# Gate product in two passes over stacked weights, and the first projection unit begun on token block 0

## The reference

```
p = x @ w_in                    # columns: pool u | q | k | v | o | i gate (4) | f gate (4)
mLSTM: log f = log_sigmoid(f + bias), cumulative sums and running maxima of i and log f per head,
       decay weights exp(...) from them, matrix memory C, normaliser n, stabiliser m
pool:  trailing-window means (2/4/8/16) minus token, per-group map, scale
mix = concat(pool, sigmoid(o) * h) @ w_out
x1  = LayerNorm(alpha*x + mix)
x2  = LayerNorm(alpha*x1 + relu(x1 @ w_ff1 + b1)^2 @ w_ff2 + b2)
```

## Time and profile before

| | us |
|---|---|
| median of 3 runs | 1200.44 |
| lowest and highest | 1200.1, 1204.38 |
| span of the profiled execution | 1202.4 |

### The profile page before, as it was taken

How to read it: one execution, slowest core, us unless ns; L and a number is a source line. 1 busy time by engine, 2 the same in 40 slices (tenths; PEclk the granted TensorE clock), 3 DMA queues, 4 the chain that set the end, 5 groups by cost and what they waited for, 6 DMA issues and landing times.

```text
span 1202.4 us, 18123 instructions
## 1 busy us (share of the span) xinstructions
PE 1168.3 (97%) x7520; PEld 1148.5 (96%) x7520; DVE 515.7 (43%) x912; ACT 370.3 (31%) x610; POOL 96.3 (8%) x110
## 2 busy tenths in 40 slices
PE   7999999999999998999999999999999999999993
PEld 6999999999888998999999999999999999999993
DVE  5612222235665785433433433433433433433457
ACT  5622433322433665212212212203203203203222
POOL 4000000010011321000000000000000000000046
PEclk9999999998999999999999999999999999999997
DMA  8321111131045540210211201201201201201012
GB/s 240 83 57 36 38 36 38 36 108 36 18 157 160 185 153 36 71 35 36 70 36 35 70 33 37 70 24 46 70 11 59 70 1 68 70 0 70 1 44 98
DMA packets 63277, 76.41 MB, mean 64 GB/s; under 512 B 3241, under 2 KB 50441, under 8 KB 63220
## 3 DMA queue, kind: packets, MB, share of 16 engines
q1 hardware_dynamic: 59676, 65.12, 17.1%
q0 software_dynamic: 3552, 10.59, 3.0%
HBM read 69.04 MB, written 6.88 MB: 63 GB/s over the span
## 4 chain that ended last, share of the span: by engine, by line
PE 86%; DVE 5%; ACT 4%; issue 2%; DMA 2%; SPq 0%; ACTq 0%; POOL 0%; DVEq 0%
PE bank L1127 84%; PE bank L1131 2%; ACT w_hi L582 1%; DMA x_nat_all<-in_x_sample 1%; ACT x_T L607 1%; DVE y_acc L1062 0%; DMA x_nat<-in_x_prompt 0%; ACT relu L639 0%; DVE ln_stats L976 0%; DVE x_lo L1010 0%; DVE ln_stats L989 0%; DVE res_nat L1000 0%; SPq L247 0%; DVE w_lo L1018 0%; DVE ln_stats L977 0%
## 5 line engine op out<-in xcount | busy, mean ns | idle before, releaser
L1127 PE MATMUL bank<-x_hi,w_hi 128*128 128x344 f32 (+1 forms) x1464 | 476.5, 326 | 4.7 <-DVE x_lo L1010 3.0
L1127 PE MATMUL bank<-x_hi,w_lo 128*128 128x344 f32 (+1 forms) x1464 | 469.1, 320 | 0.0
L1127 PE MATMUL bank<-x_lo,w_hi 128*128 128x344 f32 (+1 forms) x1464 | 468.7, 320 | 0.0
L1127 PEld LDWEIGHTS bank<-x_hi,w_hi 128*128 128x128 f32 (+1 forms) x1464 | 275.1, 188 | 12.3 <-issue 3.8
L1127 PEld LDWEIGHTS bank<-x_hi,w_lo 128*128 128x128 f32 (+1 forms) x1464 | 274.8, 188 | 1.1
L1127 PEld LDWEIGHTS bank<-x_lo,w_hi 128*128 128x128 f32 (+1 forms) x1464 | 274.7, 188 | 1.0
L1127 PE MATMUL bank<-h_hi,w_hi 128*128 128x344 f32 x768 | 246.2, 321 | 0.8
L1127 PE MATMUL bank<-h_hi,w_lo 128*128 128x344 f32 x768 | 246.2, 321 | 0.0
L1127 PE MATMUL bank<-h_lo,w_hi 128*128 128x344 f32 x768 | 246.0, 320 | 0.0
L1062 DVE TENSOR_TENSOR y_acc<-y_acc,bank 128x344 f32<-128x344 f32 x192 | 95.9, 511 | 193.0 <-PE bank L1127 193.0
L582 ACT ACTIVATE w_hi<-w_raw 128x2048 fp32r<-128x2048 f32 x31 | 59.2, 1910 | 286.4 <-PE bank L1127 286.4
(11 more groups left out here) (216 smaller groups left out, 722.3 us busy)
## 6 DMA issues: line engine op xcount, KB each, us to landing
w_raw<-in_w_ff SPq DMA_DIRECT2D x32, 1024.0 KB, 5.3
w_raw<-in_w_out SPq DMA_DIRECT2D x12, 1024.0 KB, 4.9
w_raw<-in_w_in SPq DMA_DIRECT2D x16, 512.0 KB, 5.3
x_nat_all<-in_x_prompt SPq DMA_DIRECT2D x6, 512.0 KB, 7.6
x_nat<-in_x_prompt POOLq DMA_DIRECT2D x6, 512.0 KB, 4.8
out_y_prompt<-out SPq DMA_DIRECT2D x6, 512.0 KB, 2.6
w_raw<-in_w_in SPq DMA_DIRECT2D x2, 1024.0 KB, 5.9
sample_C<-in_state_C POOLq DMA_DIRECT2D x4, 512.0 KB, 6.8
```

Of the source, the lines that this page charges most:

```text
L1127: return nc.tensor.matmul(out, lhsT, rhs, start=start, stop=stop, skip_group_check=True)
```

## The change

1. **Gate product.** The gate weights get 100 columns: high parts in rows 0 to 3 and 32 to 35, low parts in rows 64 to 67 and 96 to 99. For each slice there are two matmuls instead of three (stacked weights by x high, stacked weights by x low), 16 per block instead of 24. The result goes to bank 7. ACT copies the two low rows groups to `gate_lo`, and DVE adds them, the high rows and the bias (`gate_rows_sum`), where ACT alone wrote the rows before.
2. **Order.** Unit 1's weights are fetched ahead of tiles 3 to 8. PE's list becomes `x_block(0)`, `gates(0)`, product 0 of unit 1, `x_block(1)`, product 1, `x_block(2)`, `gates(1)`, product 2, `gates(2)`, constants, products 3 to 5. The products of unit 1 now go block by block (f = i % 2, b = i // 2). ACT's and DVE's lists follow.
3. Unit 2's `split_hi` waits for the third gate product (its slot holds the gate weights), and the row results are transposed behind unit 2's fifth product.

```diff
@@ sync @@
-            for t in range(3, len(TILES)):
-                token_dma(sp, XNAT[0:TILES[t][1], t, :], a["x_prompt"], a["x_sample"], t, True, x_in[t])
             for u in range(1, U_OUT):
                 kind, j = PROJ[u - 1]
+                if u == 2:
+                    for t in range(3, len(TILES)):
+                        token_dma(sp, XNAT[0:TILES[t][1], t, :], a["x_prompt"], a["x_sample"], t, True, x_in[t])
                 if u >= 2:
                     sp.wait_ge(lo_done, u - 1)
...
@@ scalar @@
+            def gate_lo_rows(b):
+                act.wait_ge(gate_done, b + 1)
+                if b:
+                    act.wait_ge(gate_sum, 2 * b)
+                A(GL[0:NH, 0, :], N_[64:64 + NH, 0:BLK], ACT.Copy)
+                A(GL[0:NH, 1, :], N_[96:96 + NH, 0:BLK], ACT.Copy).then_inc(gate_low, 1)
...
+            act.wait_ge(gate_sum, 2 * NBLK)
             A(TZ[0:NH, :], TF[0:NH, :], ACT.Abs).then_inc(act_row, 1)
...
@@ vector @@
+            def gate_rows_sum(b):
+                if b == 0:
+                    dve.wait_ge(bias_in, 16 * 3)
+                dve.wait_ge(gate_low, b + 1)
+                stt(TI[0:NH, blk(b)], N_[0:NH, 0:BLK], SMALL[0:NH, 0:1], GL[0:NH, 0, :], ALU.add, ALU.add).then_inc(gate_sum, 1)
+                stt(TF[0:NH, blk(b)], N_[32:32 + NH, 0:BLK], SMALL[0:NH, 1:2], GL[0:NH, 1, :], ALU.add, ALU.add)\
+                    .then_inc(gate_sum, 1)
...
@@ tensor @@
+                for k in range(KC):
+                    mm(N_[0:GATE_ROWS, 0:BLK], gslot(WH)[:, k, :], XH[:, k, blk(b)], k == 0, False)
+                    last = mm(N_[0:GATE_ROWS, 0:BLK], gslot(WH)[:, k, :], XL[:, k, blk(b)], False, k == KC - 1)
+                last.then_inc(gate_done, 1)
...
             x_block(0)
-            x_block(1)
             pe.wait_ge(lo_done, 1)
             gates(0)
+            pe.wait_ge(lo_done, 2)
+            first_unit(0)
+            x_block(1)
+            first_unit(1)
             x_block(2)
             gates(1)
+            first_unit(2)
             gates(2)
...
+            for i in range(3, 6):
+                first_unit(i)
...
-                    if u == 2 and i == 1:
+                    if u == 2 and i == 4:
```

More of the change, by code:

```diff
@@ L50 @@
 N_OUT = N_PROJ + NBLK * KC
-GATE_ROWS = 36
+GATE_ROWS = 100
 PAIRS = NCH // 2
@@ L133, in build_layer @@
         assert base + cur[0] <= nc.sbuf_usable_end, (base + cur[0], nc.sbuf_usable_end)
+        GL = at("gate_lo", [P, 2, BLK], o_lay)
         VM = at("v_masked", [P, 2, 4, P], o_lay)
@@ L162, in build_layer @@
         stT_ready, stT_read = sem("stT_ready"), sem("stT_read")
+        gate_done, gate_low, gate_sum = sem("gate_done"), sem("gate_low"), sem("gate_sum")
         act_row, dve_row = sem("act_row"), sem("dve_row")
@@ L368, in keep @@
                 for j in js:
-                    pool.wait_ge(gemm_read, N_GATE + 12 * h + 3 * j + 3)
+                    pool.wait_ge(gemm_read, N_GATE + (6 if h == 0 and j == 0 else 12 * h + 3 * j + 3))
                     G.tensor_copy(SM[:, j, h, :], QKV[h % 2][:, j, sa]).then_inc(smp_kept, 1)
@@ L441, in split_hi @@
                 act.wait_ge(raw_in[u % 2], RAW_AT[u])
-                if u >= 2:
+                if u == 2:
+                    act.wait_ge(gate_done, NBLK)
+                elif u > 2:
                     act.wait_ge(gemm_done, outputs_to(u - 2))
@@ L453, in _, with x_hi_part @@
             A(SMALL[:, 3:4], ONES[:, 0:1], ACT.Copy)
-            for s in range(2 * len(TILES)):
+            def x_hi_part(s):
                 t0, n = TILES[s // 2]
@@ L460, in _ @@
                   bank[3 + s % 4][:, :].rearrange("p (k n) -> p k n", k=4)[:, :, 0:n], ACT.Copy).then_inc(x_hi, 1)
[L461 to L474, removed]
+            def gate_lo_rows(b):
[4 more added lines that the diff above has]
+                A(GL[0:NH, 1, :], N_[96:96 + NH, 0:BLK], ACT.Copy).then_inc(gate_low, 1)
             def evac(u, i):
                 kind, j = PROJ[u - 1]
-                f, b = i // 3, i % 3
+                f, b = (i % 2, i // 2) if u == 1 else (i // 3, i % 3)
                 n = N_GATE + 6 * (u - 1) + i
@@ L491, in evac @@
                     A(Y[:, 4 + j, blk(b)], src, ACT.Sigmoid).then_inc(gemm_read, 1)
-            act.wait_ge(gemm_read, NBLK)
+            for s in range(6):
+                x_hi_part(s)
+            split_hi(0)
+            split_hi(1)
+            gate_lo_rows(0)
+            evac(1, 0)
+            for s in range(6, 12):
+                x_hi_part(s)
+            evac(1, 1)
+            for s in range(12, 18):
+                x_hi_part(s)
+            gate_lo_rows(1)
+            evac(1, 2)
+            gate_lo_rows(2)
+            act.wait_ge(stT_ready, 1)
+            A(CST[:, :], B_[:, 0:92], ACT.Copy).then_inc(stT_read, 1)
+            act.wait_ge(stT_ready, 2)
+            A(SPT[:, :, :, :].rearrange("p g b r -> p g (b r)"),
+              S_[:, :].rearrange("p (g n) -> p g n", g=4)[:, :, 0:NS * NBUF], ACT.Copy).then_inc(stT_read, 1)
+            act.wait_ge(gate_sum, 2 * NBLK)
             A(TZ[0:NH, :], TF[0:NH, :], ACT.Abs).then_inc(act_row, 1)
@@ L499, in _ @@
             A(TZ[0:NH, :], TM[0:NH, :], ACT.Ln, bias=1.0).then_inc(act_row, 1)
-            evac(1, 0)
-            evac(1, 1)
+            evac(1, 3)
             split_hi(2)
@@ L506, in _ @@
             A(RBH[0:NH, pr], TN[0:NH, pr], ACT.Copy).then_inc(act_row, 1)
-            evac(1, 2)
+            evac(1, 4)
             act.wait_ge(dve_row, ROW_Z)
@@ L547, in _ @@
                     act.wait_ge(consts, 4)
-                for i in range(3 if u == 1 else 0, 6):
+                for i in range(5 if u == 1 else 0, 6):
                     evac(u, i)
@@ L724, in after_rows @@
                 dve.wait_ge(dve_row, row_n[0])
-            V.memset(WL[:, 0, 0:KC * GATE_ROWS].bitcast(F32), 0.0)
             row(V.memset(WH[:, 0, 0:KC * GATE_ROWS].bitcast(F32), 0.0), ROW_PAD)
@@ L733, in _, with x_lo_part @@
             row(V.memset(RBL[:, :].bitcast(F32), 0.0), ROW_INV)
-            for s in range(2 * len(TILES)):
+            def x_lo_part(s):
                 t0, n = TILES[s // 2]
@@ L740, in _ @@
                                 XH[:, ks, t0:t0 + n].bitcast(F32), ALU.subtract).then_inc(x_lo, 1)
-                if s == 5:
-                    split_lo(0)
-            split_lo(1)
+            def gate_rows_sum(b):
[5 more added lines that the diff above has]
+                    .then_inc(gate_sum, 1)
+            for s in range(6):
+                x_lo_part(s)
+            split_lo(0)
+            split_lo(1)
+            gate_rows_sum(0)
+            for s in range(6, 18):
+                x_lo_part(s)
+            gate_rows_sum(1)
+            gate_rows_sum(2)
             dve.wait_ge(stT_read, 2)
@@ L1158, in gates, with unit_product, first_unit @@
                 pe.wait_ge(x_lo, 6 * b + 6)
-                split_product(bank[b][0:GATE_ROWS, 0:BLK], lambda k: gslot(WH)[:, k, :], lambda k: gslot(WL)[:, k, :],
-                              lambda k: XH[:, k, blk(b)], lambda k: XL[:, k, blk(b)], range(KC)).then_inc(gemm_done, 1)
+                if b:
+                    pe.wait_ge(gate_sum, 2 * b)
+                for k in range(KC):
+                    mm(N_[0:GATE_ROWS, 0:BLK], gslot(WH)[:, k, :], XH[:, k, blk(b)], k == 0, False)
+                    last = mm(N_[0:GATE_ROWS, 0:BLK], gslot(WH)[:, k, :], XL[:, k, blk(b)], False, k == KC - 1)
+                last.then_inc(gate_done, 1)
+            def unit_product(u, f, b, n, ks=range(KC), before=None):
+                pe.wait_ge(gemm_read, n - 2)
+                cs = slice(P * f, P * (f + 1))
+                return split_product(bank[n % 3][:, 0:BLK], lambda k: wslot(WH, u)[:, k, cs], lambda k: wslot(WL, u)[:, k, cs],
+                                     lambda k: XH[:, k, blk(b)], lambda k: XL[:, k, blk(b)], ks, before)
+            def first_unit(i):
+                n, f, b = N_GATE + i, i % 2, i // 2
+                unit_product(1, f, b, n).then_inc(gemm_done, 1)
+            pe.sem_inc(gemm_done, N_GATE)
+            pe.sem_inc(gemm_read, N_GATE)
             pe.wait_ge(consts, 1)
             x_block(0)
-            x_block(1)
             pe.wait_ge(lo_done, 1)
             gates(0)
+            pe.wait_ge(lo_done, 2)
+            first_unit(0)
+            x_block(1)
+            first_unit(1)
             x_block(2)
             gates(1)
+            first_unit(2)
             gates(2)
@@ L1245, in att3 @@
                 last.then_inc(num_ready, 1)
-            for u in range(1, U_OUT):
+            for u in range(2, U_OUT):
                 pe.wait_ge(lo_done, u + 1)
```

6 lines of the change are left out of this document (3 added, 3 removed).

## The result

| | before | after |
|---|---|---|
| median us | 1203.95 (6 runs, 1200.1 to 1204.92) | 1212.73 (6 runs, 1209.57 to 1214.94) |
| span of the profiled execution | 1202.4 | 1209.3 |

The ratio is 1.0079, with a 95% interval of 1.0057 to 1.010: slower, by 6.9 to 12 us. The forecast was 1212.1 in a range of 1207.0 to 1216.5. The kernel before measured 1203.95 over six runs, the first three among them, against the 1200.44 that the sum started from, so the difference came out smaller (9.5 us by the ratio, 8.8 by the medians) than the 11.7 forecast.

A forecast was written before the change was run, and what follows sets the result against it. PE, busy 97% of the 1202.4 us span, was taken as the bound. On the 1200.4 median, +7.7 for unit 2's later start and +4.0 for the slow clock gave 1212.1 us; range 1207.0 to 1216.5, held at 80%.

The forecast's parts named there:

- the two conditions for unit 2: PE can begin unit 2 only with unit 1 finished and unit 2's w_lo there, which before was 3.2 us early.
- Part 1: Gate in two passes: 100 columns cost no more; 8 matmuls fewer in each of 3 blocks remove 3.8 us of PE work.
- Part 2: First stretch: gate product from 10.9 to 13.4, ACT starts on unit 1's weights at 12.6, product 0 at 16.9 after 3.5 us pause.
- rival (b): SP's queue holds back unit 1's second weight transfer, delaying product 0 and all behind it: 1215.8 us; chance 0.07.
- Part 3: PE's list: last gate product ends at 39.5 against 29.2; unit 1 ends at 51.3, 1.0 us earlier than 52.3.
- Part 4: Row chain starts 10.3 us later, 0.5 added; unit 2's w_lo at 60.0, PE waits 8.7 us, +7.7 us.
- Part 5: Slow clock behind two pauses: 1.6 us for that ahead of product 0, 2.4 for the long w_lo wait, +4.0 together.
- (a): Rival: the stall comes without a slow clock, 1208.1 us; chance 0.12.
- (c): Rival: clock falls at every transpose block between products, twice more at 1.6 us: 1215.3; chance 0.03.
- (d): Rival: unit 2's w_lo is not held by the row chain; unit 2 begins at 51.3, time 1199.4; chance 0.04.

The follow-up runs named there:

- e9: e2 with 8 more matmuls ahead of each gate product, so each costs PE 24 as before the change: 1205.07 us, ratio 1.0011 to the kernel before.
- e5: Kernel before with the two-pass gate alone, the old order in all lists, second and third gate products in banks 0 and 1: 1202.36 us, ratio 0.9993.
- e2: e1 with the PSUM copies of unit 1's last two products and unit 2's first ahead of ACT's row work: 1202.21 us, ratio 0.9989.
- e7: e4 with the five transposes of constants directly behind the gate products, ahead of products 1 and 2 of unit 1: 1202.87 us, ratio 0.9992.
- e3: Changed kernel with the third gate product, in a bank of its own, ahead of product 2 of unit 1: 1211.55 us, ratio 1.0058.
- e4: e3 with product 1 of unit 1 behind the gate products too, only product 0 ahead of them: 1212.05 us, ratio 1.0076.
- e6: Changed kernel with 50 idle matmuls of 344 columns put into PE's wait for unit 2's w_lo: 1210.74 us, ratio 1.0074.
- e1: Changed kernel with unit 2's weight split (w_hi on ACT, w_lo on DVE) ahead of the row chain: 1205.14 us, ratio 1.0017.

## Why the prediction was right, point by point

**What bounds the kernel, and the two conditions for unit 2.** Right. All the difference up to unit 2's fifth product is when unit 2 begins and at what clock.

**Part 1, two passes.** Right: 100-column matmuls go at the same pace, 16 instead of 24. What they are worth depends on the pauses behind them: 2.6 us of 3.8 in e9, 0.5 in e5.

**Part 2, the first stretch.** Product 0 at 16.70 for 16.9. ACT took unit 1's weights at 12.41 in the changed kernel (I had 12.6), so rival (b), weights held up in SP's queue, did not come. SP's second issue for them lasted 4.2 us, against 8.5 before, and no semaphore wait is named for it; that a full queue holds it is likely, and no view says so. The biases landed at 19.2 as worked out, and delayed nothing there. One row of it was off: the gate product began at 11.66 and ran to 15.8, not from 10.9 to 13.4. Its matmuls start 0.29 us apart up to 14.64 and 0.157 from 14.86 on, which is the half clock and then the full one; the pause for `w_lo` hid all of that. The profile gives a granted clock of 1.00 for 9 to 14 all the same, as it does in the earlier trace rows for 4 to 9, where the first 24 transposes took 4.99 us and 8 more only 1.09. So at the very start the pace of the matmuls has to be read and not the granted clock, and the prediction's "1.00 in all stretches up to 52" says too much.

**Part 3, PE's list.** Constants at 39.13 for 39.5; `x_block` took 3.1 us each (20.58 to 23.71).

**Part 4, the row chain.** The addition by low rows and sums was guessed at 0.5 and was that: 44.95 + 1.07 - 39.13 = 6.9, against 6.4 before. From Ln to `w_lo`'s end 13.5, as before. Wait 8.43 for 8.7, shift 7.25 for 7.7. e2 and e7 show that it was this and nothing else. What the prediction had not seen is that the constants' copies on ACT are a second head of the chain; it did not matter there, since they come 0.5 us ahead of the last sum, but it decided e3 and e4.

**Part 5, the clock.** In the profiled execution its two terms were too large: 1.6 for the first pause was 0 (product 0 took 3.9 us, at full clock), and 2.4 for the long wait was 1.3 (e6 against the changed kernel). Neither is always so small: in e4, product 0 lasts from 16.66 to the transposes at 23.26, 6.6 us instead of 3.9, and the clock in it was the half one, and the long waits of e3 and e4 cost 2.6. The changed kernel's six runs lie in two groups, 1209.6 to 1211.1 and 1214.4 to 1214.9, with mean granted clocks of 0.989 to 0.990 and 0.984 to 0.985. What makes the two is open: only one of the six has a trace, and the six runs of the kernel before, which has no pause ahead of product 0, split as well (1200.1 and 1200.4, then 1203.5 to 1204.9).

**The level.** The forecast's 1212.1 and the median of 1212.73 agree partly by luck: the difference forecast (11.7) was 2.2 us over the ratio's 9.5, and the kernel before measured 3.5 us over the median of three that it was based on. Its median in the 17 to 26 runs beside the experiments, 1203.1 to 1203.4, says that those three were low. The upper end of the range, 1216.5, lies under what its own terms add up to, 1214.9 + 1.4 + 1.0 = 1217.3; nothing measured hangs on that.

**The rivals.** (a), no slow clock, did not hold, but it erred by less than the forecast's +4.0 did in the profiled execution. (c), the clock falling at every block of transposes, did not come: it stayed at full from 16.70 through both blocks to the wait, and the products behind them took 3.8 us each. Its counter-argument, that transposes alone bring the full clock, holds in the trace of before and not in this one: here the transposes of 4.78 to 10.34 were done, and a pause of 1.31 us had passed, and the gate product still began at half the pace. (d), `w_lo` free of the row chain, is what e2 built: the 1.0 us said for it was 1.3 there. The prediction weighed it with DVE "busy in nearly all" of the 19.9 us from the last gate product to `w_lo`; by the earlier trace rows DVE sat idle for 3.86 us of them while ACT did Abs, Exp and Ln, and that is the hole that e2 uses.

## What to carry to other kernels

When work is pulled ahead to fill an engine's pauses, ask what it is put ahead of: here 11 us of product went ahead of the last input of a 20 us chain, whose cover had a margin of 3 us, and the chain held something short (a 2.3 us weight split) that the filled engine needed next. The cure was not to undo the filling, but to take that short piece out from behind the chain, and then the copies that stood behind the same chain on the other engine. And the head of a chain is the last of everything in its engine's list ahead of it, also of copies that have nothing to do with it.

## What the runs showed of the hardware that was not expected

The same pause costs differently from one execution to the next. Pauses of 1.92 and 2.19 us ahead of product 0 (e1, e2) were followed by a product of 3.9 us, and pauses of 1.96 and 2.02 us (e3, e6) by one of 5.4 us (transposes at 22.22 and 22.26 behind a start at 16.8), with the half clock in it; behind 2.96 us (e4) it took 6.6 us.

A longer wait need not cost more. The wait of 8.4 us cost 1.3 us of it, those of 7.2 and 5.3 us (e3, e4) cost 2.6, and the 3.0 us wait of the earlier trace rows cost 1.6. What counts is how much of the slow stretch meets work: in the changed kernel the clock was already low in 50 to 59 (0.82), while PE did nothing, and full again from 63 on, where e3 had 0.51 in the whole of 60 to 66.
